# Modulation product: interleaved column groups in shared accumulators, row-major transfers, and fp32r row sums

## The chip, the cores and the metric

The kernel runs on one core of one Trainium2 chip. The metric is the device time of one execution in microseconds (us); the median over the runs is compared.

## The reference, cut to what matters

Two transformer blocks run one after the other on x, of 256 tokens by 2048. The change touches only how the second block gets its modulation vectors from the condition `c_2`:

```python
def second_block(x, c, ..., w_ada, b_ada, norm_mix, norm_ffn, norm_final):
    c_act = jax.nn.silu(c)
    for l in range(DEPTH):                                   # DEPTH = 1
        mod = (c_act @ w_ada[l] + b_ada[l])[:, None, :]      # w_ada: 2048 x 12288, fp32
        sh1, sc1, g1, sh2, sc2, g2 = jnp.split(mod, 6, axis=-1)
        h = rms_norm(x, norm_mix[l]) * (1.0 + sc1) + sh1
        x = x + g1 * hybrid_mixer(h, ...)
        h = rms_norm(x, norm_ffn[l]) * (1.0 + sc2) + sh2
        x = x + g2 * conv_glu_ffn(h, ...)
    return rms_norm(x, norm_final)
```

The first block (dilated attention and gated linear attention, then a gated feed-forward of width 5632) doesn't need `mod`.

## The kernel before, in words

**Order of the work.** The stages follow each other on every engine: FirstMixer, Glu (gate and up projections of the first feed-forward), Down (its down projection), SecondMixer, ConvGlu, Down again, and the final norm. Every projection is made as three fp32r products of high and low parts. SP loads a weight block of 512 KB (`load`, L245 to L253), ACT makes its high part (`split_hi`, L289), DVE its low part (`split_lo`, L297), and PE multiplies (`multiply_block`, L330; `multiply_part`, L608; Down, L1858 and L1875; SecondMixer, L2216 and L2509). ACT and DVE run three such units ahead of PE. Each engine's order is written out by hand: a stage has a loop over units ("ticks"), and each extra step stands at a fixed tick on its engine. Between engines there are only semaphores.

**The modulation product** (class `Ada`, L483) is made on the side during all of that. The 12288 columns are 12 groups ("leads" 0 to 11) of 1024. For each group SP brings w_ada in eight transfers of 1 MB (`load`, L498), two row blocks of 128 rows each, into a double buffer; DVE takes 16 steps (`product`, L516, and L518 for the first of a group), each multiplying a 128x1024 block by the 128 values of silu(c) that belong to its rows, one per partition, and adding into a 128x1024 accumulator. What is left is a sum over the 128 partitions:
- Groups 0 to 5 are accumulated one after the other in a single buffer, group 0 late in FirstMixer and the others in Glu. Their sums are taken in Glu, once in every second turn: PE transposes the accumulator in eight pieces after the turn's first unit (`turn_sums`, L458 to L460; called `mid` at L1670), and DVE reduces them (`reduce_sums`, L467) before it starts on the next group.
- Groups 6, 7 and 8 are accumulated in Down, in three buffers of their own. When SecondMixer begins, PE sums the first two by 16 matmuls with a one-column operand (`Down.ada_sums`, L1953), with the first four transposes of the block's input (L2152) between the tenth and the eleventh; DVE adds the bias at tick 6 (L1963).
- The third of those and group 9, accumulated in SecondMixer, go to DRAM and come back (1 MB) before ConvGlu. There `scale_sums` (L3609) sums one by eight one-column matmuls (L3616) and the other by eight transposes (L460), three idle transposes follow to keep PE at work (`keep_busy`, L449), and DVE finishes in `first_scales` (L3627) and, at its tick 1, in `last_scales` (L3630 to L3639), for which ACT waits at tick 2.
- Groups 10 and 11 (the gate g2) are accumulated in ConvGlu and are wanted as a row on all partitions: `row_sums` (L3641) multiplies them by a stationary matrix of ones, two fp32 matmuls of 512 columns for each group, in the middle of ConvGlu.

**The two starts.** At the start of SecondMixer and of ConvGlu PE can't go on with projections until the last 512 columns of x are there: ACT squares them, DVE forms the mean in a chain of one-column steps (L3172 to L3179; L3745 to L3749), computes 1 + scale (`modulation`, L3547), takes the reciprocal (L3183; L3754), ACT and DVE scale x (L2117, L2130), PE transposes it (L2141), and ACT and DVE add the shift and split (L2161, L2168). Only then the first unit runs.

Of the kernel before, what the change touches and what calls it, by code (L numbers as in the profile page):

```python
# [21 lines left out]
ds = bass.ds  # L22
# [38 lines left out]

COLS = {}
_n = 0
for _name, _w in (("attn_norm_w", 16), ("ffn_norm_w", 16), ("norm_mix_2", 16), ("norm_ffn_2", 16), ("c_2", 16),
# [3 lines left out]
                  ("conv_w0", 88), ("conv_w1", 88), ("conv_w2", 88), ("conv_b", 88), ("b_ada_2", 96)):  # L68
# [13 lines left out]
def constants():  # L82
# [4 lines left out]
    parts = [("ident", r == c), ("ones", np.ones((P, P))), ("headsum", same),  # L87
             ("incl", same & (r <= c)), ("anti", same & (r >= c))]
# [33 lines left out]
class Kit:  # L122

    def __init__(self, nc, ctx, ins, at):
# [28 lines left out]
        self.ada_w = [self.sem("ada_w0"), self.sem("ada_w1")]  # L154
# [302 lines left out]
def turn_sums(kit, acc, bank):  # L457

    for q in range(8):
        step = kit.nc.tensor.transpose(kit.ps[:, bank + q // 4, (q % 4) * P:(q % 4 + 1) * P], acc[:, q * P:(q + 1) * P],  # L460
                                       kit.c("ident"))
    return step

def reduce_sums(kit, a, bank):

    return kit.nc.vector.tensor_reduce(kit.modcols[:, ds(a, 8)], kit.ps[:, bank:bank + 2, :].rearrange(  # L467
        "p b (q n) -> p (b q) n", n=P), AX, ALU.add)

def add_bias(kit, a, count):

    b = COLS["b_ada_2"] + a
    cols = kit.modcols[:, a:a + count]
    kit.dve(kit.nc.vector.tensor_tensor(cols, cols, kit.col[:, b:b + count], ALU.add))

class Ada:

    def __init__(self, kit, w, acc, free=None, stored=None):  # L483

        self.kit, self.w, self.acc, self.free, self.stored = kit, w, acc, free, stored

    def load(self, sp, lead, j, m):

        kit = self.kit  # L490
        if self.free:
            sp.wait_ge(*self.free)
            self.free = None
        a = 8 * lead + m
        if a >= 2:
            sp.wait_ge(kit.ada_acc, 2 * (a - 1) + 16 * j)
        w = kit.ins["w_ada_2"][0]
# [3 lines left out]
    def product(self, dve, lead, j, s, acc=None):  # L501

        nc, kit = self.kit.nc, self.kit
        m, k = s // 2, s % 2
        if s == 0 and self.stored:
            dve.wait_ge(kit.ada_sum, lead - 1)
            dve.wait_ge(self.stored, 16)
        elif s == 0 and lead and acc is None:
            dve.wait_ge(kit.ada_sum, lead + j)
        acc = self.acc if acc is None else acc  # L510
        if k == 0:
            dve.wait_ge(kit.ada_w[m % 2], 64 * lead + 64 * j + 16 * (m // 2 + 1))
        w, c = self.w[:, m % 2, k, :], kit.cols("c_2", s)
        if s:
            dve.wait_ge(kit.ada_acc, 16 * lead + s + 16 * j)
            step = nc.vector.scalar_tensor_tensor(acc, w, c, acc, ALU.mult, ALU.add)  # L516
        else:
            step = nc.vector.tensor_scalar(acc, w, c, None, ALU.mult)  # L518
        step.then_inc(kit.ada_acc, 1)

    def sums(self, pe, lead, j, bank=6):

        nc, kit = self.kit.nc, self.kit
        pe.wait_ge(kit.ada_acc, 16 * lead + 16 * j)
        if lead > 1:
            pe.wait_ge(kit.ada_out, lead - 1 + j)
        for q in range(8):
            step = nc.tensor.matmul(kit.ps[:, bank, q:q + 1], lhsT=self.acc[:, q * P:(q + 1) * P],
                                    rhs=kit.c("ones")[:, 0:1], start=True, stop=True)
        step.then_inc(kit.ada_sum, 1)  # L530

    def turned(self, pe, lead, j, bank=6):

        kit = self.kit
        pe.wait_ge(kit.ada_acc, 16 * lead + 16 * j)
        if lead > 1:
            pe.wait_ge(kit.ada_out, lead - 1 + j)
        turn_sums(kit, self.acc, bank).then_inc(kit.ada_sum, 1)

    def reduced(self, dve, lead, j, bank=6):  # L540

        kit = self.kit
        dve.wait_ge(kit.ada_sum, lead + j)
        reduce_sums(kit, 8 * (lead - 1) + 8 * j, bank).then_inc(kit.ada_out, 1)

    def copy(self, dve, lead, j, bank=6):

        kit = self.kit
        dve.wait_ge(kit.ada_sum, lead + j)
        a = 8 * (lead - 1)  # L550
        kit.nc.vector.tensor_tensor(kit.modcols[:, ds(a + 8 * j, 8)], kit.ps[:, bank, 0:8],
                                    kit.col[:, ds(COLS["b_ada_2"] + a + 8 * j, 8)], ALU.add).then_inc(kit.ada_out, 1)

# [59 lines left out]
def small_vectors(kit):  # L613
# [8 lines left out]
    def src(name):  # L622
# [9 lines left out]
        if name == "conv_b":  # L632
            return ins["ffn_conv_b_2"].rearrange("a (r f) -> (a r) f", f=P)
        return ins[name].rearrange("a (r f) -> (a r) f", f=P)

    packs = [names[0:1], names[1:14], names[14:19], ["conv_w0"], ["conv_w1"], ["conv_w2"], ["conv_b"], ["b_ada_2"]]
    rows = []
    for names_ in packs:
        at, of = 0, []
        for name in names_:  # L640
            w = width[name]
            if name in ("mu_wd", "mu_wa"):
                a = c3 + (DRANK if name == "mu_wa" else 0)
                of.append((at, at + 1, DRANK, mu[0:1, a:a + DRANK]))
# [3291 lines left out]
```

## Time and profile before

| | |
|---|---|
| median of 3 runs | 2351.09 us (2350.31 to 2352.11) |
| the profiled execution, its own time | 2352.51 us |
| span in its profile | 2350.7 us |
| PE (matmuls) busy | 2337.8 us, 99% |
| PE weight loads busy | 2151.6 us, 92% |
| DVE busy | 1616.4 us, 69% |
| ACT busy | 1153.2 us, 49% |
| moved by DMA | 543.62 MB, 231 GB/s on the mean |

The busy time of PE overlaps with its weight loads and its ends are modelled, so a share of 99% says that PE was hardly ever waiting, not that it worked at its peak. The chain of waits is the view that says what an instruction costs: it gives each stretch of PE from its start to the start of the next.

### The profile page before, as it was taken

How to read it: one execution, taken by the hardware profiler on the slowest of the kernel's cores; microseconds unless marked ns; L12 is line 12 of the kernel's file. 1: busy time of each engine (PE TensorE's matmuls, PEld its weight loads, DVE VectorE, ACT ScalarE, POOL GpSimd, SP SyncE). 2: the span in 40 equal slices, each digit the busy share in tenths (PEclk: the TensorE clock that was granted, in tenths of full speed). 3: DMA queues.
4: the chain of work that ended last, by engine and by line, in shares of the span. 5: the costliest groups of instructions: out<-in, count | busy, mean ns of one | idle time of the engine just before them, and what ended most of it. 6: DMA issues, size and time to landing. Idle time of an engine off the chain costs nothing.

```text
span 2350.7 us, 43754 instructions
## 1 busy us (share of the span) xinstructions
PE 2337.8 (99%) x17937; PEld 2151.6 (92%) x17937; DVE 1616.4 (69%) x1931; ACT 1153.2 (49%) x1510; POOL 5.1 (0%) x7
## 2 busy tenths in 40 slices
PE   9999999999999999999999999999999999999998
PEld 8889778999999999888999899888999999998887
DVE  5668568777777766877778455667878666665556
ACT  5565454534344344444764444546544445454444
POOL 0000000000000000000000000000000000000000
PEclk9999999999999999999999999999999999999999
DMA  8556567888888877898577545555778656665563
GB/s 308 167 179 197 159 234 271 278 282 297 282 282 295 282 242 263 316 324 315 175 279 269 163 130 153 196 200 187 283 255 295 208 179 206 196 206 197 192 192 117
DMA packets 233049, 543.62 MB, mean 231 GB/s; under 512 B 15610, under 2 KB 22596, under 8 KB 232260
## 3 DMA queue, kind: packets, MB, share of 16 engines
q1 hardware_dynamic: 232756, 540.97, 68.3%
q8 instruction: 110, 1.80, 0.3%
q10 hardware_dynamic: 144, 0.52, 0.1%
q14 instruction: 39, 0.32, 0.0%
HBM read 535.11 MB, written 6.32 MB: 230 GB/s over the span
## 4 chain that ended last, share of the span: by engine, by line
PE 98%; DVE 0%; ACT 0%; issue 0%; DMA 0%; SPq 0%; DVEq 0%; ACTq 0%
PE ps L330 37%; PE ps L1858 18%; PE ps L608 18%; PE ps L2216 16%; PE ps L1875 2%; PE ps L2509 0%; PE ps L1041 0%; PE ps L1053 0%; PE ps L1071 0%; PE ps L1083 0%; PE ps L2141 0%; PE ps L460 0%; PE ps L2744 0%; PE ps L1134 0%; PE ps L2921 0%
## 5 line engine op out<-in xcount | busy, mean ns | idle before, releaser
L297 DVE TENSOR_TENSOR weights_lo<-raw_weights,weights_hi 128x1024 fp32r<-128x1024 f32 x786 | 957.6, 1224 | 659.8 <-ACT weights_hi L289 658.0
L289 ACT ACTIVATE weights_hi<-raw_weights 128x1024 fp32r<-128x1024 f32 x782 | 827.2, 1062 | 1086.8 <-PE ps L330 446.4
L516 DVE SCALAR_TENSOR_TENSOR ada_acc<-ada_w,col,ada_acc 128x1024 f32<-128x1024 f32 x180 | 230.2, 1279 | 0.1
L330 PE MATMUL ps<-conv_x_hi,weights_hi 128*128 128x256 f32 x1280 | 198.0, 277 | 0.0
L330 PE MATMUL ps<-glu_x_hi,weights_hi 128*128 128x256 f32 x1280 | 197.7, 276 | 0.0
L330 PE MATMUL ps<-glu_x_hi,weights_lo 128*128 128x256 f32 x1280 | 197.2, 276 | 0.0
L330 PE MATMUL ps<-glu_x_lo,weights_hi 128*128 128x256 f32 x1280 | 197.2, 276 | 0.0
L330 PE MATMUL ps<-conv_x_lo,weights_hi 128*128 128x256 f32 x1280 | 197.2, 276 | 0.0
L330 PE MATMUL ps<-conv_x_hi,weights_lo 128*128 128x256 f32 x1280 | 197.2, 276 | 0.0
L330 PEld LDWEIGHTS ps<-conv_x_hi,weights_hi 128*128 128x128 f32 x1280 | 169.1, 188 | 1.0 <-issue 1.0
L330 PEld LDWEIGHTS ps<-glu_x_hi,weights_hi 128*128 128x128 f32 x1280 | 169.0, 188 | 0.0
L330 PEld LDWEIGHTS ps<-glu_x_lo,weights_hi 128*128 128x128 f32 x1280 | 168.9, 188 | 0.0
L330 PEld LDWEIGHTS ps<-glu_x_hi,weights_lo 128*128 128x128 f32 x1280 | 168.9, 188 | 0.0
L330 PEld LDWEIGHTS ps<-conv_x_hi,weights_lo 128*128 128x128 f32 x1280 | 168.9, 188 | 0.0
L330 PEld LDWEIGHTS ps<-conv_x_lo,weights_hi 128*128 128x128 f32 x1280 | 168.9, 188 | 0.0
L2216 PE MATMUL ps<-m_x_hi,weights_hi 128*128 128x256 f32 (+1 forms) x576 | 94.9, 288 | 0.1
L3800 DVE SCALAR_TENSOR_TENSOR conv_y<-ps,conv_taps,conv_y 128x255 f32<-128x255 f32 (+1 forms) x176 | 72.7, 476 | 29.8 <-ACT conv_y L3732 28.8
L2216 PE MATMUL ps<-m_x_lo,weights_hi 128*128 128x256 f32 (+1 forms) x576 | 89.8, 279 | 0.0
L2216 PE MATMUL ps<-m_x_hi,weights_lo 128*128 128x256 f32 (+1 forms) x576 | 89.2, 277 | 0.5 <-issue 0.5
L1858 PE MATMUL ps<-weights_hi,down_hi 128*128 128x512 f32 x288 | 89.0, 390 | 0.5 <-DVE stat L3804 0.2
L1858 PE MATMUL ps<-weights_hi,down_lo 128*128 128x512 f32 x288 | 88.7, 389 | 0.0
L1858 PE MATMUL ps<-weights_lo,down_hi 128*128 128x512 f32 x288 | 88.7, 389 | 0.0
(560 smaller groups left out, 3635.3 us busy)
## 6 DMA issues: line engine op xcount, KB each, us to landing
raw_weights<-in_w_in_dram SPq DMA_DIRECT2D x202, 512.0 KB, 5.0
ada_w<-in_w_ada_dram SPq DMA_DIRECT2D x96, 1024.0 KB, 6.1
raw_weights<-in_w_ffn_up_dram SPq DMA_DIRECT2D x176, 512.0 KB, 4.6
raw_weights<-in_w_gate_dram SPq DMA_DIRECT2D x88, 512.0 KB, 4.6
raw_weights<-in_w_up_dram SPq DMA_DIRECT2D x88, 512.0 KB, 4.6
raw_weights<-in_w_down_dram SPq DMA_DIRECT2D x88, 512.0 KB, 5.7
raw_weights<-in_w_ffn_down_dram SPq DMA_DIRECT2D x88, 512.0 KB, 4.3
raw_weights<-in_w_out_dram SPq DMA_DIRECT2D x64, 512.0 KB, 5.1
```

What stands on the lines that cost most here:

```text
L289: kit.nc.scalar.activation(kit.slots(n, i)[0], raw, ACT.Copy).then_inc(kit.w_hi, 1)
L297: kit.nc.vector.tensor_tensor(lo, raw, hi.bitcast(F32), ALU.subtract).then_inc(kit.w_lo, 1)
L330: ins = nc.tensor.matmul(out, lhsT=lhsT, rhs=rhs, start=start and m == 0, stop=(k == KT - 1 and m == 2), skip_group_check=True)
L516: step = nc.vector.scalar_tensor_tensor(acc, w, c, acc, ALU.mult, ALU.add)
L608: ins = nc.tensor.matmul(out, lhsT=lhsT, rhs=rhs, start=start and m == 0, stop=ends and m == 2, skip_group_check=True)
L1858: ins = nc.tensor.matmul(kit.ps[:, 4 * t + 2 * half + q, :], lhsT=lhsT, rhs=rhs, start=(k == 0 and m == 0), stop=ends and m == 2, skip_gro ...
L1875: ins = nc.tensor.matmul(kit.ps[:, 4 * t + 2 * half + q, :], lhsT=lhsT, rhs=w[:, q * UN:(q + 1) * UN], start=False, stop=k == w_tiles - 1 ...
L2216: ins = nc.tensor.matmul(out, lhsT=lhsT, rhs=rhs, start=start and m == 0, stop=ends and m == 2, skip_group_check=True)
L3800: nc.vector.scalar_tensor_tensor(y[:, j, q, b:S], self.tile(j, q)[:, 0:S - b], taps[:, j, tap, q:q + 1], y[:, j, q, b:S], ALU.mult, ALU.ad ...
```

## The change

**Shared accumulators.** A transfer no longer brings 128 rows of one group. For groups 0 to 7 (columns 0 to 8191) a step takes 16 rows and all eight groups: partition 8r+g holds the 1024 columns of row r in group g. 128 such steps cover the 2048 rows, all into one accumulator ("oct"). Groups 8 and 9 go the same way with 64 rows and two groups, 32 steps, "half". Groups 10 and 11 stay as they were. The number of steps (192), their size and their ticks stay; the scalars are other columns of silu(c) (`c_oct`, `c_half`). Each 1 MB transfer has become two of 512 KB. The sum over the partitions is now one matmul per 128 columns with a mask of eight (or two) columns, which gives all eight groups at once.

```diff
+    def source(self, lead, j, s):
+        w = self.kit.ins["w_ada_2"][0]
+        if lead < 8:
+            rows = w[ds(OCT * (16 * lead + s) + 16 * OCT * j, OCT), 0:16 * UN]
+        elif lead < 10:
+            rows = w[HALF * (16 * (lead - 8) + s):HALF * (16 * (lead - 8) + s + 1), 16 * UN:20 * UN]
+        else:
+            rows = w[P * s:P * (s + 1), 2 * UN * lead:2 * UN * (lead + 1)]
+        return rows.rearrange("r (g n) -> r g n", n=2 * UN)
...
-        sp.dma_start(self.w[:, m % 2, :, :], w[2 * m * P:2 * (m + 1) * P, ds(2 * UN * lead + 2 * UN * j, 2 * UN)]
-                     .rearrange("(k p) n -> p k n", p=P)).then_inc(kit.ada_w[m % 2], 16)
+        for s in (2 * m, 2 * m + 1):
+            sp.dma_start(self.w[:, m % 2, s % 2, :], self.source(lead, j, s)).then_inc(kit.ada_w[m % 2], 16)
...
+        if s == 0 and lead in (0, 8, 10, 11):
+            step = nc.vector.tensor_scalar(acc, w, c, None, ALU.mult)
+        else:
             dve.wait_ge(kit.ada_acc, 16 * lead + s + 16 * j)
+            step = nc.vector.scalar_tensor_tensor(acc, w, c, acc if prior is None else prior, ALU.mult, ALU.add)
...
+    def sums(self, pe, bank, mask, acc):
+        kit, (a, b) = self.kit, self.kit.at[mask]
+        n = b - a
         for q in range(8):
+            step = kit.nc.tensor.matmul(kit.ps[:, bank, n * q:n * (q + 1)], lhsT=acc[:, q * P:(q + 1) * P],
+                                        rhs=kit.c(mask), start=True, stop=True)
         step.then_inc(kit.ada_sum, 1)
```

**Glu.** No sum is left to take there: `mid`, the eight transposes and the reduction are gone; DVE copies the group's 16 scalars instead.

```diff
-            mid = (lambda: self.ada.turned(pe, self.lead, j)) if summed else None
...
-            multiply_block(kit, pe, x, "T", 0, first, i, uses[0], mid)
+            multiply_block(kit, pe, x, "T", 0, first, i, uses[0])
...
-                if summed and s == begun:
-                    self.ada.reduced(dve, self.lead, j)
                 if half is not None and s % 2 == begun:
-                    self.ada.product(dve, self.lead, j, 8 * half + s // 2)
+                    q = 8 * half + s // 2
+                    if q == 0:
+                        a = COLS["c_oct"] + 16 * self.lead
+                        dve.wait_ge(kit.ada_acc, 16 * self.lead + 16 * j)
+                        nc.vector.tensor_copy(self.c_turn[:, :], kit.col[:, ds(a + 16 * j, 16)]).then_inc(self.s_c, 1)
+                        dve.wait_ge(self.s_c, 1 + j)
+                    self.ada.product(dve, self.lead, j, q, c=self.c_turn[:, q:q + 1])
```

**Start of SecondMixer.** Eight matmuls of eight columns take the place of 16 of one column; DVE adds the bias in its chain of the norm, since sh1 and sc1 are now in the same sum.

```diff
         pe.wait_ge(self.squares_in, 8)
-        self.down.ada_sums(pe, 0)
-        self.down.ada_sums(pe, 1, 0, 2)
+        self.down.ada_sums(pe)
         pe.wait_ge(self.squares_in, 11)
         for k in range(4):
             self.turned.turn_early(pe, k)
-        self.down.ada_sums(pe, 1, 2, 8)
         for k in range(4):
             self.turned.turn(pe, k)
...
+        self.down.ada_summed(dve)
         modulation(kit, 0)
...
-        if n == 6:
-            self.down.ada_reduced(dve)
-        if n == 9:
-            dve.wait_ge(kit.ada_out, self.lead - 1)
```

On PE at the start of SecondMixer, before (each row is the line, the operation, output<-operands and the tile):

```order
L1875 MATMUL ps<-down_last_lo,glu_x_hi 128x512
L1875 MATMUL ps<-down_last_hi,glu_x_lo 128x512
L1953 MATMUL ps<-cst,ada_acc_98 128x1 x8
L1953 MATMUL ps<-cst,ada_acc_99 128x1 x2
L2152 MATMUL ps<-cst,m_scaled_126 128x128 x4
L1953 MATMUL ps<-cst,ada_acc_99 128x1 x6
L2141 MATMUL ps<-cst,m_scaled_126 128x128 x4
L2216 MATMUL ps<-m_x_hi,weights_hi 96x256
```

and now, where L514 is the matmul of `sums`, and L2145, L2134 and L2209 are the old L2152, L2141 and L2216:

```order
L1879 MATMUL ps<-down_last_lo,glu_x_hi 128x512
L1879 MATMUL ps<-down_last_hi,glu_x_lo 128x512
L514 MATMUL ps<-cst,ada_acc_oct 128x8 x8
L2145 MATMUL ps<-cst,m_scaled_128 128x128 x4
L2134 MATMUL ps<-cst,m_scaled_128 128x128 x4
L2209 MATMUL ps<-m_x_hi,weights_hi 96x256
```

Ahead of the first four transposes stand eight sum matmuls where ten stood, and none stands between them and the next four, where six did.

**Start of ConvGlu.** Eight matmuls of two columns; the eight transposes and `last_scales` are gone, and with them ACT's wait at tick 2.

```diff
-        turn_sums(kit, mixer.accs[:, 1, :], 2).then_inc(kit.ada_sum, 1)
...
-        self.first_scales(dve)
+        self.scales(dve)
...
-        dve.wait_ge(kit.ada_out, self.lead - 1)
-        modulation(kit, 1, 0, 8)
+        modulation(kit, 1)
...
-                            self.last_scales(dve)
+                            nc.vector.memset(kit.stat[:, 59:60], 0.0).then_inc(kit.pair_free[1], 1)
```

On PE there, before:

```order
L2509 MATMUL ps<-weights_hi,rw_out_lo 128x512
L2152 MATMUL ps<-cst,conv_scaled_214 128x128 x4
L3616 MATMUL ps<-cst,ada_accs_back 128x1 x8
L460 MATMUL ps<-cst,ada_accs_back 128x128 x8
L449 MATMUL ps<-cst 128x128 x3
L2141 MATMUL ps<-cst,conv_scaled_214 128x128 x4
L608 MATMUL ps<-conv_x_hi,weights_hi 128x256 x8
```

and now (L454 is `keep_busy`, L580 the old L608):

```order
L2496 MATMUL ps<-weights_hi,rw_out_lo 128x512
L2145 MATMUL ps<-cst,conv_scaled_216 128x128 x4
L514 MATMUL ps<-cst,ada_acc_back 128x2 x8
L454 MATMUL ps<-cst 128x128 x3
L2134 MATMUL ps<-cst,conv_scaled_216 128x128 x4
L580 MATMUL ps<-conv_x_hi,weights_hi 128x256 x8
```

The eight transposes of the accumulator have gone from between the sums and `keep_busy`.

**Row sums.** ACT makes a high part of the accumulator and once a rounded matrix of ones, DVE a low part, three and one units before PE needs them; four fp32r matmuls take the place of two fp32 ones.

```diff
-            step = nc.tensor.matmul(kit.ps[:, 4 + 2 * g + b, :], lhsT=kit.c("ones"),
-                                    rhs=self.ada.acc[:, b * UN:(b + 1) * UN], start=True, stop=True)
+            for acc in (self.acc_hi, self.acc_lo):
+                step = nc.tensor.matmul(kit.ps[:, 4 + 2 * g + b, :], lhsT=self.ones[:, :], rhs=acc[:, b * UN:(b + 1) * UN],
+                                        start=acc is self.acc_hi, stop=acc is self.acc_lo)
```

**Smaller parts.** Two more row tables for silu(c) are loaded at the start of the kernel (two small transfers, two broadcasting copies on DVE, one more transpose on PE, two short Silu activations on ACT); one accumulator fewer goes to DRAM and back; the load of the final norm's weight moves from the start of Down to its twelfth pair of units, and PE's wait for the modulation sums at the start of Down is gone.

## Rows read from the trace of the kernel before

**Rows 1.** The page: busy time by engine, and the chain that ended last.
```profile
PE 2337.8 (99%) x17937; PEld 2151.6 (92%) x17937; DVE 1616.4 (69%) x1931; ACT 1153.2 (49%) x1510; POOL 5.1 (0%) x7
PE 98%; DVE 0%; ACT 0%; issue 0%; DMA 0%; SPq 0%; DVEq 0%; ACTq 0%
```
**Rows 2.** Waits of PE, longest first: what for, us, times, longest.
```profile
PE ps L945 <- DMA pack<-in_attn_norm_w_dram: 3.0, 1, 3.0
```
**Rows 3.** Groups: busy us, mean ns, then idle before and its releaser.
```profile
L297 DVE TENSOR_TENSOR weights_lo<-raw_weights,weights_hi 128x1024 fp32r<-128x1024 f32 x786 | 957.6, 1224 | 659.8 <-ACT weights_hi L289 658.0
```
**Rows 4.** Chain of waits in Glu: start us, us, what.
```profile
427.93 0.87 PE ps L460 x8
...
514.28 0.87 PE ps L460 x8
515.16 87.12 PE ps L330 x768
...
866.24 0.87 PE ps L460 x8
```
**Rows 5.** Chain of waits in Down.
```profile
908.12 217.87 PE ps L1858 x960
```
**Rows 6.** Chain of waits in ConvGlu, the first of two row sums.
```profile
1731.91 1.72 PE ps L3646 x4
```
**Rows 7.** Chain of waits at the start of SecondMixer.
```profile
1147.75 2.12 PE ps L1953 x20
...
1150.37 2.08 PE ps L1953 x12
1152.45 0.95 PE ps L2141 x4
...
1153.47 4.81 PE ps L2216 x24
```
**Rows 8.** Timeline at the start of SecondMixer, ACT.
```profile
1150.44 0.71 ACT L2117 ACTIVATE m_scaled<-x_weighted,stat 128x512 f32<-128x512 f32 x1
```
**Rows 9.** Windows there: PE, PEld, DVE, ACT, POOL busy, clock (PEclk), DMA share, GB/s.
```profile
1149.00:1150.00 1.00, 1.00 (x11) 1.00 (x12) 0.86 (x6) 0.93 (x5) 0.00 (x0) 1.00 0.00 0
...
1151.00:1154.00 3.00, 2.94 (x14) 2.57 (x15) 1.40 (x5) 1.34 (x4) 0.00 (x0) 0.50 0.99 249
...
1157.50:1158.00 0.50, 0.50 (x6) 0.50 (x5) 0.50 (x1) 0.00 (x0) 0.00 (x0) 1.00 0.09 33
```
**Rows 10.** Chain of waits at the start of ConvGlu.
```profile
1614.25 0.93 PE ps L460 x8
1615.18 0.33 PE ps L449 x3
...
1620.13 0.44 PE ps L2141 x4
```
**Rows 11.** Timeline there, DVE, ACT and PE.
```profile
1614.36 0.17 DVE L3627 TENSOR_TENSOR modcols<-ps,col 128x8 f32<-128x8 f32 x1 [0.50 <-PE ps L3616]
...
1614.74 0.71 ACT L2117 ACTIVATE conv_scaled<-x_rows,stat 128x512 f32<-128x512 f32 x1
...
1615.63 0.68 PE L2141 MATMUL ps<-cst,conv_scaled 128*128 128x128 f32 x4
1616.64 0.71 PE L608 MATMUL ps<-conv_x_hi,weights_hi 128*128 128x256 f32 x4 [0.33 <-issue]
```
**Rows 12.** Windows there, same columns.
```profile
1615.00:1617.00 2.00, 1.55 (x12) 1.07 (x11) 1.54 (x5) 1.47 (x4) 0.00 (x0) 1.00 1.01 408
```
**Rows 13.** The page: DMA issues, KB each, median us to landing.
```profile
ada_w<-in_w_ada_dram SPq DMA_DIRECT2D x96, 1024.0 KB, 6.1
...
raw_weights<-in_w_gate_dram SPq DMA_DIRECT2D x88, 512.0 KB, 4.6
```
**Rows 14.** Windows, the end of FirstMixer's output projection and Glu, same columns.
```profile
330.00:345.00 15.00, 14.84 (x68) 11.96 (x68) 11.34 (x17) 8.73 (x11) 0.00 (x0) 1.00 1.04 394
...
470.00:900.00 430.00, 430.00 (x3794) 430.00 (x3793) 314.29 (x264) 175.57 (x167) 0.00 (x0) 1.00 0.80 277
```

More of the change, by code:

```diff
@@ L153, in __init__ @@
             self.sem(n) for n in ("weights_hi", "weights_lo", "act_hi", "act_lo"))
-        self.ada_w = [self.sem("ada_w0"), self.sem("ada_w1")]
+        self.ada_w = [self.sem(f"ada_w{n}") for n in range(2)]
         self.ada_acc, self.ada_sum, self.ada_out = (self.sem("ada_" + n) for n in ("acc", "sum", "out"))
@@ L454, in spread @@
     return kit.nc.tensor.transpose(out, col.broadcast_to([P, P]), kit.c("ident"))
[L457 to L468, printed above, removed]
@@ L503, in product, with scalar @@
+    def scalar(self, lead, s):
+        name, first = ("c_oct", 0) if lead < 8 else ("c_half", 8) if lead < 10 else ("c_2", lead)
+        return self.kit.cols(name, 16 * (lead - first) + s)
+    def product(self, dve, lead, j, s, acc=None, prior=None, c=None):
         nc, kit = self.kit.nc, self.kit
         m, k = s // 2, s % 2
[L505 to L509, printed above, removed]
@@ L540, in reduced, with summed @@
[L540 to L552, printed above, removed]
+    def summed(self, lead, bank, mask):
+        kit, (a, b) = self.kit, self.kit.at[mask]
+        n, first, bias = b - a, 8 * lead, COLS["b_ada_2"] + 8 * lead
+        cols, add = (x.rearrange("p (g q) -> p q g", q=8) for x in (kit.modcols[:, first:first + 8 * n],
+                                                                    kit.col[:, bias:bias + 8 * n]))
+        return kit.nc.vector.tensor_tensor(cols, kit.ps[:, bank, 0:8 * n].rearrange("p (q g) -> p q g", g=n), add, ALU.add)
@@ L944, in turn_pack @@
         _, w, _ = self.packs[n]
-        kit.nc.tensor.transpose(kit.ps[:, 6, 0:w], self.pack[0:w, n, :], kit.c("ident")[0:w, 0:w]
-                                ).then_inc(self.s_packT, 1)
+        last = n == len(self.packs) - 1
+        if n >= len(self.packs) - 2:
+            pe.wait_ge(self.s_cwide, 2)
+        rows = self.pack[0:w, 0 if last else n, :]
+        kit.nc.tensor.transpose(kit.ps[:, 6, 0:w], rows, kit.c("ident")[0:w, 0:w]).then_inc(self.s_packT, 1)
     def spread_scale(self, at):
@@ L1945, in tail_lo, with ada_sums, ada_summed @@
         kit.nc.vector.tensor_tensor(lo, raw_half(kit, m), hi.bitcast(F32), ALU.subtract).then_inc(kit.w_lo, 1)
[L1947 to L1964 removed]
+    def ada_sums(self, pe):
+        pe.wait_ge(self.kit.ada_acc, 128)
+        self.ada.sums(pe, 0, "oct", self.accs[0])
+    def ada_summed(self, dve):
+        dve.wait_ge(self.kit.ada_sum, 1)
+        self.ada.summed(0, 0, "oct").then_inc(self.kit.ada_out, 1)
+        dve.wait_ge(self.kit.ada_out, 1)
     def act_tile(self, k, i):
@@ L3610, in scale_sums @@
     def scale_sums(self, pe):
-        kit, mixer = self.kit, self.mixer
-        pe.wait_ge(mixer.s_accs, 16)
-        pe.wait_ge(kit.pair_free[0], self.uses[0] + 1)
-        for q in range(8):
-            step = kit.nc.tensor.matmul(kit.ps[:, 1, q:q + 1], lhsT=mixer.accs[:, 0, q * P:(q + 1) * P],
-                                        rhs=kit.c("ones")[:, 0:1], start=True, stop=True)
-        step.then_inc(kit.ada_sum, 1)
-        pe.wait_ge(mixer.s_xlast, ST)
-        turn_sums(kit, mixer.accs[:, 1, :], 2).then_inc(kit.ada_sum, 1)
@@ L3648, in row_sums, with acc_split @@
         step.then_inc(kit.ada_sum, 1)
+    def acc_split(self, i, j, u, after):
+        g, off = divmod(16 * i + 8 * j + u - 36 - after, self.GROUP) if isinstance(i, int) else (0, 1)
+        return g if off == 0 and 0 <= g < 2 else None
     def sync(self, sp):
@@ L3722, in body @@
                         self.turned.scale_first(act, 3 + u // 2)
+                    g = self.acc_split(i, j, u, 1)
+                    if g is not None:
+                        act.wait_ge(kit.ada_acc, 16 * (self.lead + g + 1))
+                        if g == 0:
+                            nc.scalar.activation(self.ones[:, :], kit.c("ones"), ACT.Copy)
+                        else:
+                            act.wait_ge(kit.ada_sum, 2 + g)
+                        nc.scalar.activation(self.acc_hi[:, :], self.ada.acc, ACT.Copy).then_inc(self.s_acchi, 1)
                     if (j, u) == (1, 3):
@@ L3825, in program @@
         junk = t("y_squares", 80, [P, ST, D])
-        accs = [t(f"ada_acc_{6 + n}", a, [P, 2 * UN])[:, :] for n, a in enumerate((56, 60, 106))]
+        accs = [t(f"ada_acc_{n}", a, [P, 2 * UN])[:, :] for n, a in (("oct", 56), ("half", 60))]
         def wide_head(w):
```

198 lines of the change are left out of this document (88 added, 110 removed).

## The prediction

> **What bounds the kernel now.** I read the page first: PE is busy for 2337.8 of 2350.7 us, and 98% of the chain that ended last is PE [rows 1]. The waits of PE come next: the longest is 3.0 us, once, at the start of the kernel [rows 2], and the others are half a microsecond or less. Then the groups of DVE, to see who paces whom: weights_lo is idle 659.8 us before its instructions and waits 658.0 of them for ACT's high part [rows 3], which in its turn waits for PE to give a weight buffer back. DVE and ACT follow PE, and the transfers follow them. So the kernel is bound by PE's own row of instructions: one that is taken out of a stretch where PE never stops gives back its whole length, and one taken out where PE stands waiting for the norm of x gives nothing. The question for each part is thus where it stands, and the chain of waits tells it, because it counts from one start to the next.
>
> **The change part by part.**
>
> Glu's transposes. The chain of Glu reads 87.12 us of projections, 0.87 us of transposes, and so on, without a gap [rows 4]. Six groups had their transposes there: five in the rolled turns (the first at 514.28, the last at 866.24) and one at 427.93. They are gone, and nothing replaces them on PE: 6 x 0.87 = 5.2 us. The cover could only fail if something else were late at once. DVE has 314.29 of 430 us of work in this stretch [rows 14]; it loses a reduction per group and gains a copy of 16 columns and a first step that adds as well. That is below its idle time, so −5.2 stands whole.
>
> Row sums. One of the two sums takes 1.72 us in the chain [rows 6]; the other reads the same. The new form is four fp32r matmuls of 512 columns. Down makes 960 of these in 217.87 us [rows 5], 0.227 each, so four cost 0.91, and each sum saves 0.81: −1.6 us. The high and low parts are one pass each over 128x1024, by ACT and DVE, 1.2 us like a weight block's low part [rows 3]. They stand one or more units ahead of PE (87.12 / 32 = 2.7 us each [rows 4]), on engines that wait for PE. I cost them at nothing; without that cover they would cost up to 1.2 us each.
>
> Start of SecondMixer. PE takes 2.12 us for ten sum matmuls, four transposes, 2.08 us for six more, and only then starts the transposes of the last quarter at 1152.45 [rows 7]. What these need was ready earlier: ACT's scaled columns end at 1150.44 + 0.71 = 1151.15 [rows 8]. The start of ConvGlu has the same steps, and there the transposes begin 0.9 us after ACT's scaling began (1615.63 against 1614.74 [rows 11]). Put on 1150.44 this gives 1151.33, 1.1 us ahead of 1152.45. DVE however gets the bias step into its chain behind L3179: 0.17 us for such a step [rows 11] and a wait; against that, removing the queue on PE may let the transposes start by 1151.2. The gain is between 0 (if the added step and its waits, some 0.2 us each way, were longer than the rows say and DVE's last piece is what PE waits for) and 1.3; I take −1.1, nearest to the start of ConvGlu, which is the same code.
>
> The clock at that place. It was granted in full until 1150, at half from 1151 on, and in full again from 1157.5 [rows 9]; before it fell PE had done one-column matmuls and four transposes since 1147.75. What half the clock costs I read from the other start, which had it in full [rows 12]: four transposes take 0.95 against 0.44 us, and the first unit 4.81 against 1620.13 − 1616.64 = 3.49 [rows 7, 10, 11], in all 1.8 us. With the change the thin stretch is shorter but has an idle piece of over a microsecond in it. I let the clock fall there as before: 0.
>
> Start of ConvGlu. The transposes are 0.93 us of the chain and `keep_busy` 0.33 [rows 10], but what ends them is not what lets the next step run: DVE's bias step waits for the sums at 1614.36, ACT scales from 1614.74, and PE's next transposes begin at 1615.63 [rows 11]. So the 0.93 us turn into waiting. The bias step is now waited for before the mean, +0.15; `last_scales` leaves DVE and ACT's wait for it goes, −0.2 at most, where ACT and DVE alternate with PE from unit to unit. Sum 0, between −0.3 and +0.3.
>
> The start of the kernel. One more transpose of a table on PE, priced as an eighth of 0.87, and a wait at the tick of the last table: +0.1 to +0.5, I take +0.2. The longer chain of small loads on SP lies in front of weight blocks that wait in their buffers for some microseconds. The moved load of the final norm's weight, the accumulator that no longer goes out, and the eight first steps that now add as well as multiply lie beside PE: 0.
>
> Transfers. 96 of 1 MB, 6.1 us to landing, become 192 of 512 KB; a block of that size lands in 4.6 us [rows 13]. Two at once can't be slower than two in a row, 9.2 us, nor faster than the 6.1 of one alone would suggest by much, so a pair costs −0.5 to +3.1 us of landing. In Glu a group has eight pairs in 88 us and two buffers, so a pair is asked for 11 us ahead of its use; hence 0.
>
> **Sum:** −5.2 − 1.6 − 1.1 + 0 + 0.2 = −7.7 us. The profiled execution took 2352.5 us and goes to 2344.8; it lies 1.4 us above the median of the three, and since medians are compared I take 2351.1 − 7.7 = **2343.4 us**.
>
> **A rule that bears on it.** The trace shows PE at the full clock through the start of ConvGlu, with eight transposes and three idle ones between the sums and the next work [rows 10, 12]. The Trainium skill ("TensorE: Matmul & The Clock Gate", Part 4) says that PE's transposes don't count as busy time for the clock in the way matmuls do. By that rule the removal of eight of them can't make the clock fall, and the sum stays; by the rows, where the only thin stretch without them is the one at whose end the clock fell, it might, +1.8 us. This is the first rival.
>
> **The rivals.**
> - *The clock falls at ConvGlu.* After the change that start has eight two-column matmuls, three transposes and about a microsecond of idling, much like the start at which it fell. For it: PE's busy time in 1615 to 1617 is already 1.55 of 2 us [rows 12], and the change takes away 0.93 more before it. Against: the stretch is shorter than the one at SecondMixer, and ordinary matmuls follow within two microseconds of `keep_busy`. The price is 1.8 us: 2345.2. Chance 0.22.
> - *The clock no longer falls at SecondMixer*, because the thin stretch has shrunk from 4.7 us (1147.75 to 1152.45) to about 3.5. −1.8: 2341.6. Chance 0.10.
> - *The gain is given back at the edges*: no gain at the start of SecondMixer (+1.1), the low clock at ConvGlu (+1.8), and the first two pairs of smaller transfers pushing out weight blocks where the DMA share is 1.04 and PE already loses 0.16 us in 15 [rows 14], up to 3.1 us each. That gives 2347 to 2352, no change that can be told. Chance 0.11.
> - *Glu becomes bound by transfers: slower.* Its DMA share is 0.80 at 277 GB/s [rows 14]. Each group brings 8.4 MB in a stretch of 88 us in which 277 x 88 = 24.4 MB move, so w_ada has a third of the share, 0.27. If halving the transfers made them cost twice the time on the engines, the share would be 1.07, and the five stretches of 88 us would stretch by 7%, 31 us: 2374 us. It begins at a rise of 75% (0.20 / 0.27) and outweighs the gain of 7.7 us at 82%. Against it: two landings in a row, 9.2 against 6.1 us [rows 13], are a rise of 51% and give 0.94. A 512 KB weight block is the size of most other transfers here, and they keep up. Chance 0.05. The Trainium skill ("DMA: Bandwidth & Descriptors", the table of sizes and its rule) advises transfers of 1 MiB or more and has a fixed cost for each; it speaks against this edit, and the trace agrees so far that 512 KB takes more than half of the time of 1 MB.
> - *The change doesn't do what it says on PE* (the transposes' time was hidden). The chain excludes it nearly: all stretches before and after are PE. It is within the third case.
>
> **How the numbers follow.** The forecast has 0.52, the rivals 0.22, 0.10, 0.11 and 0.05. A measurement of this kernel can tell about 0.2%, 4.7 us, from no change: faster means below 2346.4, slower above 2355.8. The forecast and the first two rivals are faster: 0.84; the third is the same: 0.11; the fourth slower: 0.05. The range takes in the forecast's own bounds (start of SecondMixer 0 to −1.3, ConvGlu ±0.3, tables +0.1 to +0.5, together −0.6 to +1.7), both clock cases, and half a microsecond to a microsecond for the runs, which spread by 1.8: 2340.5 to 2347.0.
>
> **What the profile of the changed kernel would show.** Right: Glu's chain one unbroken stretch of projections; four row-sum matmuls in 0.9 us; at the start of SecondMixer PE's transposes of the last quarter some 1.1 us earlier after the last matmul of Down, with idle time before them ended by ACT or DVE; no wait of PE longer than half a microsecond elsewhere; the new transfers landing within about 6 us. Wrong: waits of weights_lo or of the products for ada_w, or PE waiting for weights_lo in Glu; a stretch at half the clock at the start of ConvGlu, or none at SecondMixer; row sums preceded by a wait for the low part; a start of ConvGlu that got shorter, which would mean that PE's queue and not the norm of x had ended last there.

## The result and the profile after

The changed kernel takes 2412.3 us (median of four runs, 2409.67 to 2415.26) where the one before takes 2351.6 in the same session: ratio 1.0259, 95% interval 1.0241 to 1.0277. It is 61 us slower. The forecast was 2343.4 us, in a range of 2340.5 to 2347.0. The execution whose profile follows took 2415.26 us; its span is 2413.5.

The page: busy time, the chain that ended last by engine, and two of the DMA issues (KB each, median us to landing).

```profile
PE 2351.8 (97%) x17866; PEld 2157.3 (89%) x17866; DVE 1604.2 (66%) x1930; ACT 1154.4 (48%) x1515; POOL 5.1 (0%) x7
...
PE 71%; DMA 17%; DVE 7%; issue 2%; SPq 1%; ACT 1%; DVEq 0%; ACTq 0%
...
ada_w<-in_w_ada_dram SPq DMA_DIRECT2D x192, 512.0 KB, 8.0
...
raw_weights<-in_w_gate_dram SPq DMA_DIRECT2D x88, 512.0 KB, 11.6
```

The chain was PE for 98% [rows 1]; now transfers hold 17% of it. A transfer of w_ada has half the bytes and takes 8.0 us from issue to landing in place of 6.1, and the weight blocks that share the queue with it have gone from 4.6 to 11.6 us [rows 13].

Windows of Glu and Down, and of the last part of Down, in which groups 8 and 9 are loaded (columns as in rows 9: the last three are the granted clock, the DMA share and GB/s).

```profile
470.00:900.00 430.00, 403.71 (x3444) 398.94 (x3444) 284.78 (x248) 160.32 (x153) 0.00 (x0) 0.98 0.94 263
900.00:1148.00 248.00, 229.43 (x1172) 194.46 (x1172) 162.20 (x163) 97.41 (x119) 0.10 (x1) 0.97 0.91 263
...
1125.00:1180.00 55.00, 55.00 (x244) 45.58 (x243) 46.26 (x49) 24.27 (x30) 0.00 (x0) 1.00 0.94 350
```

In Glu the DMA engines are busy for 0.94 of the time and move 263 GB/s; before they needed 0.80 for 277 [rows 14]. Per byte that is 24% more engine time (0.94 / 263 against 0.80 / 277). The third line is the same kernel with transfers of 64 rows by two groups: 0.94 for 350 GB/s, no dearer than before. It has w_ada's transfers almost alone, so the comparison per byte is rough; the times of single packets below make it exact. So it is not the change's transfers as such, but those of groups 0 to 7.

Waits of PE and of DVE in 430 to 910 us (what for, us, times, longest).

```profile
PE ps L335 <- DVE weights_lo L302: 26.1, 20, 2.4
```

```profile
DVE ada_acc L506 <- DMA ada_w<-in_w_ada_dram: 156.3, 39, 6.2
```

The chain of waits in Glu, one of its rounds (start us, us, what):

```profile
583.39 2.28 DVE weights_lo L302 x2
585.83 0.37 SPq L258
586.46 0.55 SPq L487
587.21 15.38 DMA ada_w<-in_w_ada_dram
```

The same chain where Down's matmuls begin and where they have ended (DVE's first step of the next norm):

```profile
945.53 11.19 PE ps L1862 x48
...
1212.92 0.70 DVE x_rows L2079
```

Before, DVE never waited for ada_w. Now it waits 39 times in Glu, and since it works in order, the low parts of the weights queue behind the product that waits; PE waits for those. Both are signs that the prediction had named for being wrong. The time lost shows by stage. Down's first matmul began at 908.12 us; it now begins at 945.53, when the forecast's gains had put it at 903: 42 us lost up to the end of Glu. The waits of PE shown above make most of it, and after several of them the clock fell for a while (0.98 on the mean in the first window). Down's matmuls took 239.6 us (908.12 to 1147.75 [rows 5, 7]); they now take 267.4 (945.5 to 1212.9): 28 us. DVE waits for w_ada there another 15 times, 58.9 us in all.

### The profile page after: what moved, and what is told of

Its sections match the earlier page's. It is cut to its first block, busy times and chain, and to the rows that moved or that the text cites. A ratio compares the mean times of both kernels' runs of the same rounds, so it can differ in the third digit from the quotient of the medians.

```text
span 2413.5 us, 43781 instructions
## 1 busy us (share of the span) xinstructions
PE 2351.8 (97%) x17866; PEld 2157.3 (89%) x17866; DVE 1604.2 (66%) x1930; ACT 1154.4 (48%) x1515; POOL 5.1 (0%) x7
## 4 chain that ended last, share of the span: by engine, by line
PE 71%; DMA 17%; DVE 7%; issue 2%; SPq 1%; ACT 1%; DVEq 0%; ACTq 0%
PE ps L335 21%; DMA ada_w<-in_w_ada_dram 16%; PE ps L2209 15%; PE ps L580 15%; PE ps L1862 12%; DVE weights_lo L302 4%; PE ps L1879 2%; DVE ada_acc L506 1%; SPq L487 1%; DVE ada_acc_oct L506 1%; DMA raw_weights<-in_w_out_dram 1%; PE ps L2496 0%; SPq L258 0%; PE ps L1026 0%; PE ps L1038 0%
## 5 line engine op out<-in xcount | busy, mean ns | idle before, releaser
L506 DVE SCALAR_TENSOR_TENSOR ada_acc<-ada_w,glu_c,ada_acc 128x1024 f32<-128x1024 f32 x80 | 102.5, 1282 | 161.0 <-DMA ada_w<-in_w_ada_dram 156.3
L2209 PE MATMUL ps<-m_x_hi,weights_hi 128*128 128x256 f32 (+1 forms) x576 | 95.0, 288 | 0.1
L2209 PE MATMUL ps<-m_x_lo,weights_hi 128*128 128x256 f32 (+1 forms) x576 | 89.2, 277 | 0.0
L2209 PE MATMUL ps<-m_x_hi,weights_lo 128*128 128x256 f32 (+1 forms) x576 | 88.9, 277 | 0.0
## 6 DMA issues: line engine op xcount, KB each, us to landing
raw_weights<-in_w_gate_dram SPq DMA_DIRECT2D x88, 512.0 KB, 11.6
```

What stands on the lines that cost most here:

```text
L506: step = nc.vector.scalar_tensor_tensor(acc, w, c, acc if prior is None else prior, ALU.mult, ALU.add)
L2209: ins = nc.tensor.matmul(out, lhsT=lhsT, rhs=rhs, start=start and m == 0, stop=ends and m == 2, skip_group_check=True)
```

## The experiments

All were timed against the kernel before in the same sessions, whose median was 2351.3 to 2352.5 us. The second, fifth, sixth, eighth and tenth experiment form other modulation vectors than the reference, from other rows of w_ada; they are there for their time only. Two theories stood at the start. **A**: the addresses and the form of the new transfers cost the time. **B**: it is their number, 192 in place of 96.

**One transfer cut in two, and nothing else.**

```diff
-        sp.dma_start(self.w[:, m % 2, :, :], w[2 * m * P:2 * (m + 1) * P, ...].rearrange("(k p) n -> p k n", p=P))
+        for s in (2 * m, 2 * m + 1):
+            sp.dma_start(self.w[:, m % 2, s % 2, :], w[s * P:(s + 1) * P, ...])
```

> The kernel before, with each 1 MB transfer of w_ada cut into two of 512 KB and nothing else. Theory A (what costs the 60 us is the addresses: 16 rows of eight groups each): no change, 2351 to 2354 us, the Glu window keeps a DMA share of about 0.80. Theory B (twice as many transfers, each with a cost of its own): 2395 us or more, with Glu's DMA share above 0.93 and DVE waiting for ada_w.

Measured: 2351.6 us, ratio 0.9998 (0.9988 to 1.0007), landing in 5.2 us. B falls: 512 KB transfers in twice the number cost nothing here, and the DMA share in Glu is 0.81.

**The change with the old addresses.**

```diff
-            rows = w[ds(OCT * (16 * lead + s) + 16 * OCT * j, OCT), 0:16 * UN]
+        rows = w[P * s:P * (s + 1), ds(2 * UN * lead + 2 * UN * j, 2 * UN)]
```

> The changed kernel, all else kept, but each 512 KB transfer reads 128 rows of one group of 1024 columns, as before (the modulation vectors are then other numbers; the work is the same). Theory A (addresses): the changed kernel's gain shows at last, 2343 to 2346 us. Theory B (number of transfers): stays at 2410 us.

Measured: 2345.31 us (2344.58 to 2346.26), ratio 0.9971 (0.996 to 0.9981). Everything else in the change is together worth about what was forecast, 7.2 us (4.5 to 9.4 by the interval); all of the loss is in the transfers. Its chain of waits, in Glu, at the starts of SecondMixer and ConvGlu, and one of the row sums:

```profile
467.79 432.49 PE ps L335 x3816
...
1142.77 0.70 DVE x_rows L2074
...
1146.41 0.67 PE ps L2129 x4
...
1147.42 4.62 PE ps L2204 x24
1152.03 0.44 PE ps L2129 x4
...
1605.29 0.44 PE ps L2140 x4
...
1610.08 5.34 PE ps L575 x24
1615.42 0.44 PE ps L2129 x4
...
1726.98 0.92 PE ps L3610 x4
```

Glu is one unbroken stretch of projections. These lines are used again below.

**Rows far apart.** Sixteen rows and eight groups as in the change, the rows 128 apart.

```diff
-            rows = w[ds(OCT * (16 * lead + s) + 16 * OCT * j, OCT), 0:16 * UN]
+            t = w.rearrange("(r t) n -> t r n", t=P)[ds(16 * lead + s + 16 * j, 1), :, 0:16 * UN]
+            return t.rearrange("a r (g n) -> (a r) g n", n=2 * UN)
```

> The changed kernel with 16 rows and eight groups in each transfer of groups 0 to 7 as now, rows still outermost, but the rows lie 128 apart instead of side by side (scalars to match, read in single elements at the start of the kernel, which may cost some us there). Theory A1 (neighbouring rows, read by the 16 DMA engines at once, disturb each other in the memory): faster than 2380 us. Theory A2 (what costs is that a row's eight pieces, 32 KB on end, go to eight neighbouring partitions one after the other): stays at 2410 us. Theory B: stays at 2410 us.

Measured: 2415.97 us, ratio 1.0286 (1.0261 to 1.031). Where the rows lie in memory doesn't matter: A1 falls.

**The group outermost.**

```diff
-        return rows.rearrange("r (g n) -> r g n", n=2 * UN)
+        return rows.rearrange("r (g n) -> g r n", n=2 * UN)
```

> The changed kernel with the same rows and columns in each transfer, but the group outermost: partition 16g+r (64g+r for groups 8 and 9) in place of 8r+g, masks and scalars to match. Theory A1 (which rows lie side by side in one transfer): stays near 2410 us. Theory A2 (order of the pieces in a transfer): back to 2343 to 2346 us, if the pieces of a group, 48 KB apart, go as those of the kernel before. Theory B: stays at 2410 us.

Measured: 2822.84 us, ratio 1.2032 (1.1976 to 1.2088). The same bytes, and a loss nearly eight times as large: I had expected one theory to leave it at 2410 and the other to mend it, and it did neither. The windows say what the outermost dimension does. Glu, and the stretch with groups 8 and 9, whose outermost dimension is here only two:

```profile
470.00:900.00 430.00, 359.91 (x2949) 354.21 (x2948) 243.82 (x212) 138.06 (x133) 0.00 (x0) 0.95 0.73 226
...
1270.00:1400.00 130.00, 59.05 (x208) 45.99 (x206) 31.25 (x32) 20.11 (x25) 0.00 (x0) 0.74 0.32 104
```

PE starves while the DMA engines on the mean are busy for 0.73, and for 0.32. These are the durations of all packets of 4 KB in 470 to 900 us of each trace, where they are those of w_ada, and, in the last row, in 1125 to 1180 us:

| kernel | outermost by inner | mean ns | median ns |
|---|---|---|---|
| before | 128 | 166 | 159 |
| changed | 16 by 8 | 269 | 275 |
| rows apart | 16 by 8 | 268 | 274 |
| old addresses | 128 | 173 | 159 |
| changed, groups 8 and 9 | 64 by 2 | 176 | 159 |

The packets themselves take 62% longer than before, 55% longer than with the old addresses. They do so in a crowd of the same size: with twelve or more of them in flight the median is 279 ns in the changed kernel and 159 in the one before.

The mean share of 0.94 hides a second thing. During 0.33 of this stretch of the changed kernel exactly one 4 KB packet is in flight, against 0.06 before and 0.04 with the old addresses. It looks as if the last packets of a transfer came one after the other on one engine that trails, while the others are busy with weight blocks, and a product can't start before the last one. Which engine it would be, and why one trails, no row shows.

The same page (The descriptor swizzle) says that a plain transfer of 128 partitions is dealt out so that each engine writes partitions of one port of SBUF only, four and the four that lie 32 further on. The page doesn't say which partitions an engine gets when the source is 16 by 8. If it is one row of eight pieces, the engine writes eight neighbouring partitions, which by that map belong to two ports, each shared with another engine. This supposition became **theory D** (the form of the transfer), against **theory M** (the memory side).

**The old rows, written with two dimensions.** The 512 KB that a transfer reads are those of the second experiment.

```diff
         rows = w[P * s:P * (s + 1), ds(2 * UN * lead + 2 * UN * j, 2 * UN)]
+        if lead < 8:
+            return rows.rearrange("(b a) n -> a b n", a=16)
```

> As the second experiment (128 rows of one group in each transfer, so the same 512 KB of addresses; the modulation vectors are other numbers), but for groups 0 to 7 the source is written with two dimensions, 16 by 8 rows, so that partition 8a+b gets row a+16b. Theory D (the form: an outermost dimension of 16 hands each DMA engine eight neighbouring partitions, and two engines then write by the same way into SBUF): as slow as the changed kernel, 2405 to 2415 us, with packets of 4 KB near 275 ns. Theory M (memory side: eight pieces of one row, or 16 rows at once): 2345 us, packets of 159 ns.

Measured: 2423.97 us (2411.75 to 2444.9), ratio 1.0336 (1.0289 to 1.0383); packets 266 ns on the mean, median 271, exactly one in flight for 0.31 of the stretch. One line that only regroups 128 rows as 16 by 8 brings back all of the loss. M falls.

**Every third piece, one dimension of 128.**

```diff
+            pieces = w.rearrange("r (q t n) -> (r q) t n", t=3, n=2 * UN)
+            return pieces[ds(32 * (16 * lead + s) + 512 * j, P), lead % 3, :]
```

> The changed kernel, but for groups 0 to 7 a transfer takes every third piece of 4 KB, 128 of them: 32 rows of four groups, interleaved on the partitions as the change does with 16 rows of eight, but written with a single dimension of 128 (some pieces are read twice and others never, so the modulation vectors are other numbers). Theory D: 2343 to 2347 us, since interleaving as such costs nothing when the outermost dimension is 128. Theory M: slower than 2380 us.

Measured: 2345.37 us, ratio 0.9973 (0.9962 to 0.9984), packets 171 ns. Interleaving groups on the partitions costs nothing if one dimension of 128 says it.

**32 by 4 in place of 16 by 8.** The changed kernel's own last transfers (64 rows by two groups, above) were fast though they too have a second dimension.

```diff
-            return rows.rearrange("(b a) n -> a b n", a=16)
+            return rows.rearrange("(b a) n -> a b n", a=32)
```

> The fifth experiment (128 rows of one group in each transfer, source with two dimensions, other modulation vectors) with 32 by 4 rows in place of 16 by 8. If the outermost dimension of 16 is the cause alone: 2345 us with packets of 159 ns. If any second dimension is: above 2400 us.

Measured: 2345.34 us, ratio 0.9973 (0.9962 to 0.9984), packets 182 ns on the mean, median 159, exactly one in flight for 0.03 of the stretch. So a second dimension as such costs nothing; 16 by 8 does. (With 128 partitions an outermost dimension of 16 and an inner one of eight come together, and no run parts them.) The window of Glu in the fifth experiment (16 by 8) and in this one (32 by 4):

```profile
470.00:900.00 430.00, 405.32 (x3485) 400.44 (x3484) 289.13 (x252) 161.69 (x154) 0.00 (x0) 0.99 0.93 265
```

```profile
470.00:900.00 430.00, 430.00 (x3796) 430.00 (x3795) 313.45 (x264) 177.60 (x168) 0.00 (x0) 1.00 0.82 279
```

**What is left without new transfers.** The kernel before, with fp32r row sums and a rearranged start of SecondMixer; `fill` is an fp32 matmul of 256 columns.

```diff
         self.down.ada_sums(pe, 0)
+        fill(kit, 1)
         self.down.ada_sums(pe, 1, 0, 2)
...
-        self.down.ada_sums(pe, 1, 2, 8)
+        fill(kit, 1)
         for k in range(4):
             self.turned.turn(pe, k)
...
+                if n == 0:
+                    self.down.ada_sums(pe, 1, 2, 8)
```

> The kernel before with the old transfers and the old transposes in Glu, the row sums of the change (fp32r, -1.6 us), and at the start of SecondMixer only ten sum matmuls and the four early transposes before the last quarter's transposes (-1.1 us), with two fp32 matmuls of 256 columns among them to keep the clock up; the other six sum matmuls go behind the first unit (+1.3 us). If the fill holds the clock (-1.8 us): 2348 us. If the clock falls all the same: 2350 us. It tells what is left of the change without the new transfers.

Measured: 2349.4 us, ratio 0.999 (0.9981 to 0.9999), a little faster. It lies between the 2348 and the 2350 expected, so the time doesn't tell whether the fill held the clock; the profile does: the first unit of SecondMixer took 2.52 us, with the clock at 1.00.

```profile
1153.46 2.52 PE ps L2222 x20
```

```profile
1152.00:1155.00 3.00, 2.48 (x19) 2.07 (x19) 2.48 (x7) 3.00 (x7) 0.00 (x0) 1.00 0.80 194
```

The mean granted clock of a whole execution is on record for every one, and a fall at a start lowers it by about a thousandth. It is 0.999 in all eleven of this experiment. In those of the kernel before it is 0.999 in 20 of 67 (median 2351.1 us), 0.998 in 35 and 0.997 in 12 (2352.7 us). So before, too, the clock seems to have held in some executions, and a fill gains less on the median than what a fall costs.

**Fill at both starts**, on top of the second experiment.

```diff
         self.down.ada_sums(pe)
+        fill(kit, 1, 1)
...
             self.turned.turn_early(pe, k)
+        fill(kit, 2, 1)
...
-                keep_busy(kit, 3, 7, S)
+                fill(kit, 3, 7)
```

> The second experiment (old addresses, 2345.3 us) with fp32 matmuls of 256 columns in the waits of both starts: three at SecondMixer, and three in place of the idle transposes at ConvGlu. In the second experiment the clock stood at half after both. If such matmuls hold it where the thin sums and transposes did not: -1.8 us at SecondMixer and -2.1 at ConvGlu, 2341.5 us. If the idle time decides: no change.

Measured: 2343.47 us (2342.86 to 2343.7), ratio 0.9964 (0.995 to 0.9977), 1.8 us under the second experiment where 3.9 was expected if the clock held. The windows of the first units of both starts, in the second experiment:

```profile
1149.00:1152.00 3.00, 3.00 (x21) 3.00 (x20) 2.97 (x5) 1.54 (x3) 0.00 (x0) 0.69 0.35 135
...
1610.00:1613.00 3.00, 2.94 (x14) 2.96 (x14) 2.89 (x7) 3.00 (x6) 0.00 (x0) 0.50 0.27 106
```

and with the fill:

```profile
1149.00:1152.00 3.00, 2.90 (x26) 2.69 (x24) 3.00 (x5) 2.48 (x5) 0.00 (x0) 1.00 0.31 95
...
1610.00:1613.00 3.00, 2.93 (x27) 2.72 (x26) 2.97 (x5) 2.46 (x5) 0.00 (x0) 1.00 0.00 0
```

The clock held at both, and the two starts of this execution are 1.2 and 2.1 us shorter, up to the transposes of the second unit; that unit then gives back 0.3 us at each. The two profiled spans differ by 3.0 us (2344.1 and 2341.1), the medians by 1.8. The profiled execution lies 0.6 us above its median there and 0.5 below it here. The mean clock is 0.997 in six executions of the second experiment, 0.998 in two, and 0.999 in all five of this one, so a fall can have been missing there in few of them. Why the medians gain less than the two starts stays open.

**A version with the gain and without the loss.** Groups 0 and 1 as 64 rows by two groups, 2 to 5 as 32 by four, 6 to 9 as 64 by two; PE transposes an accumulator once in Glu. One fill stands at the start of SecondMixer and three at the start of ConvGlu.

```diff
+        if lead == 1 and not isinstance(j, int):
+            rows = w[ds(QUAD * (s - 16) + 16 * QUAD * j, QUAD), 4 * UN:12 * UN]
+        elif lead < 10:
+            a = HALF * (16 * (lead % 2) + s)
+            rows = w[a:a + HALF, 4 * UN * (lead // 2):4 * UN * (lead // 2 + 1)]
...
         body(1, 0, 1, False)
+        if between:
+            between(eng)
```

> A version of the change without an outermost dimension of 16: groups 0 and 1 as 64 rows by two groups (summed by eight transposes in Glu, once), groups 2 to 5 as 32 rows by four groups in one accumulator, groups 6 and 7, and 8 and 9, again as 64 by two; 512 KB transfers as in the change. The 64-by-two transfers of the changed kernel had packets of 159 ns, so theory D is sharpened: only 16 rows are too few, since with 32 or more each engine's eight partitions are no longer neighbours. Then: 2351.8 - 4.4 (five of six transpose groups) - 1.6 (row sums) - 0.3 (start of SecondMixer, with four sum matmuls moved behind the first unit) - 1.8 (fill that holds the clock) + 0.5 (tables) = 2344 us. If 32 rows by four groups are as slow as 16 by eight: above 2380 us.

Measured: 2346.72 us (2345.11 to 2348.44), ratio 0.9976 (0.9967 to 0.9985). It beats both kernels, but is short of the 2344 expected. In the profiled execution, which is the slowest of the eleven (2348.44 us), one fill didn't hold the clock at SecondMixer. The mean clocks part the eleven cleanly: it is 0.998 in six executions (2346.72 to 2348.44 us) and 0.999 in five (2345.11 to 2345.83). So one fill held the clock in some five of eleven. Chain of waits there in the profiled one:

```profile
1151.04 4.13 PE ps L2248 x20
1155.17 0.79 PE ps L521 x8
```

**A second fill in it.**

```diff
-        self.down.shift_sums(pe, 0, 4)
+        self.down.shift_sums(pe, 0, 2)
+        fill(kit, 1, 1)
```

> The ninth experiment, in which one fill did not hold the clock at SecondMixer (half speed from 1152 us): two of the four sum matmuls behind the early transposes give place to a second fill, and six instead of four follow the first unit. If two fills hold the clock, as in the seventh and eighth experiments: -1.8 + 0.4, so 1.4 us under the ninth, 2345.3 us, and the granted clock of 1152 to 1155 us is 1.00. If not: +0.4, 2347.1 us.

Measured: 2345.72 us (2345.38 to 2346.05), ratio 0.9974 (0.9964 to 0.9983). The chain there, and the window of 1152 to 1155 us:

```profile
1149.46 2.54 PE ps L2248 x20
1151.99 1.23 PE ps L521 x12
```

```profile
1152.00:1155.00 3.00, 3.00 (x28) 3.00 (x29) 2.33 (x4) 1.46 (x4) 0.00 (x0) 1.00 0.45 121
```

The clock is at 1.00. The unit costs 2.54 in place of 4.13 us, and 0.4 goes to the longer row of sums; the median is 1.0 us lower, less than the two intervals can part. The ten executions all have a mean clock of 0.999 and lie where the five such of the ninth experiment lay: the second fill makes regular what was chance. This is the fastest version here that computes the reference: 6 us, 0.26%, under the kernel before.

## Why the prediction was wrong

**The step that failed is the one on transfers**: "Two at once can't be slower than two in a row, 9.2 us", "a pair is asked for 11 us ahead of its use; hence 0". It priced the new transfers by rows of other ones of the same size (4.6 us, [rows 13]). Size was not what changed: the first experiment shows that halving it costs nothing, and the fifth that the same bytes from the same rows cost over 65 us when they are written as 16 by 8. The bound of 9.2 us for a pair was no bound. In the chain of the changed kernel the w_ada transfer takes 15.4 us from issue to landing, more than the 11 us ahead at which a pair is asked for. The term stood at 0 and measured +67 us (2412.3 against the 2345.3 of the second experiment).

**The slower rival had the place and the way in which the loss comes about, with the wrong cause and a chance of 0.05.** It asked for a rise of 75% in w_ada's time on the DMA engines before Glu becomes bound by them. The packets rose by 62%, which makes 0.80 + 0.27 x 0.62 = 0.97 of the engines' time; the window shows 0.94 and PE already starved. The mean over 16 engines hides what the product waits for, the last packet of a transfer, and those seem to trail here. It looked only at Glu (31 us forecast, about 42 found) and forgot Down, which lost another 28 of its 240 us to the same transfers. The rule of the Trainium skill that I weighed, on transfers of 1 MiB or more, is not what decided: by the first experiment, halving them cost nothing here. The Trainium skill's rule on the outermost dimension wouldn't have warned either, since 16 gives all 16 engines by it. But I had the source's new form before me in the diff, and no row of the kernel before had a transfer of that form; the term should have been called unknown and not 0.

**The rest of the sum was right within a microsecond or so**, as the second experiment shows, with 2345.3 us and these lines:
- Glu's transposes, −5.2: Down's first matmul moved from 908.12 to 903.08, −5.0. The tables at the start of the kernel are in it; their term was +0.2.
- Row sums, −1.6: four matmuls in 0.92 us against 1.72 [rows 6], −0.8 each. In the changed kernel they read 0.93.
- Start of SecondMixer, −1.1: from the last matmul of Down to the last quarter's transposes 1142.77 to 1146.41, 3.64 us, against 4.70 [rows 7]: −1.1. The clock fell there as forecast. What a fall costs was put at 1.8 us; by the eighth experiment it is 1.2 at SecondMixer.
- Start of ConvGlu, 0, and the first rival, +1.8 with a chance of 0.22: the rival happened. From the early transposes to the second unit's, 1605.29 to 1615.42 makes 10.1 us, against 8.0 before (1612.13 to 1620.13): +2.1. The changed kernel shows it too (first unit 4.15 us at 1680.53). The rows decided and not the Trainium skill's rule that transposes don't count: without the eight of them the clock fell. Idle time came in their place, though, so the runs don't tell whether they had counted as work or only kept PE from idling.

With the first rival the forecast was 2345.2, 5.9 us under the kernel before; the second experiment is 7.2 us under it in the same session, and its profiled span is 6.6 us shorter. The four terms make −5.6; most of the other microsecond came between the two starts, where no term stood (1152.03 to 1605.29 is 453.3 us, and 453.9 before). That 2345.3 meets 2345.2 is therefore luck in part. The answer was off by 69 us, because one term was set to zero on evidence that didn't fit it.

## What to carry to other kernels

When a transfer's access pattern changes, compare its dimensions with before, the outermost above all, and not only its bytes: into 128 partitions, sources with an outermost dimension of 128, 64 and 32 ran alike here, 16 cost 62% more per packet, and 8 and 2 left engines idle. (Only the source was varied.) The check is quick, since packet durations (159 against 275 ns) and DMA share per GB/s move at once. And a change that gains by taking work off the engine that bounds should be timed with its transfers and its instructions apart: here they were worth −7 and +67 us.

## What the runs showed of the hardware

- A transfer of 512 KB into 128 partitions whose source is 16 by 8 pieces of 4 KB has packets of 266 to 269 ns on the mean against 166 to 182 for one of 128, 64 by 2 or 32 by 4. For 0.31 to 0.33 of Glu exactly one such packet is in flight, against 0.03 to 0.06 with 128 or 32 by 4. The Trainium skill ("SBUF — State Buffer", Door 1: The DMA port swizzle) has the map of partitions to ports by which two engines would share each port in the 16-by-8 case, if an engine gets eight neighbouring partitions. Where the rows lie was excluded. Which partitions an engine gets, and the ports themselves, show in no row: that part stays an inference, and for 32 by 4 and 64 by 2 it isn't worked out.
- Work put into a start's waits held PE's clock there. In all six profiled starts with two or three fp32 matmuls of 256 columns the granted clock stayed at 1.00 (2.4 GHz). With one of them it went to 0.50 (1.2 GHz) in the profiled execution, and by the mean clocks in six of eleven. With sums, transposes and idle time alone it went to 0.50 as well, except at the start of ConvGlu before, where eight more transposes filled the wait.
